# Modulation sums of a two-block network as rows in TensorE's 32-column tiles instead of folds on VectorE

## The chip, the core and the metric

One core of a Trainium2 chip runs the whole program in one launch. TensorE multiplies, VectorE and ScalarE work element by element (VectorE also sums and transposes blocks), GpSimd adds and issues DMAs, SyncE issues DMAs. The metric is the device time of one execution in microseconds (us); less is better.

## The reference, cut to what matters

A hybrid network over 256 tokens of 2048 features: a first block (stick-breaking attention and retention, modulated by a vector `c`), then two further layers and a last norm. The change concerns the first block's modulation and norm:

```python
mod = jax.nn.silu(c) @ w_ada[layer] + b_ada[layer]      # w_ada: 2048 x 6144
shift, scale, gate = jnp.split(mod, 3, axis=-1)
h = rms_norm(x, norm_gain[layer]) * (1.0 + scale[:, None, :]) + shift[:, None, :]
proj = h @ w_in[layer]
...
x = x + (gate[:, None, :] * y).astype(x.dtype)
```

All of it is float32.

## The kernel before

**Products.** Every matrix product is cut into chunks of 1024 columns of weights (for instance 4 x 256 columns of four groups of 128 input features). SyncE loads a chunk into one of seven places of `raw` (L453, waiting until the chunk seven before is used). ScalarE writes its high half `w_hi` (`split_hi`, L469; five places, so it waits for the chunk five before), VectorE the low half `w_lo` (`split_lo`, L478), and TensorE multiplies high by high and low, low by high (L544 to L546 where the result is by tokens, L552 and L554 where it is by features). A finished block of the sum `psG` is taken out by ScalarE (L512, L513, L515, L519) and VectorE (L1357, L1374, L1385). ScalarE and VectorE are three chunks ahead of TensorE (`AHEAD`).

**The order of the work** is written by hand: each engine walks through the same list of chunks ("units"), and at each position (`p` even: in front of or within a chunk; odd: behind it) a hook may add other instructions. In the first 72 units (`mem_hook_1`, `mem_tail_hook` and `early_hook`) ScalarE and VectorE run the hook of unit u behind the split of chunk u + 3, TensorE its own behind the products of chunk u. What a hook waits for holds up all that its engine has queued behind it.

- Units 0 to 31 (`G_MEM`): keys and values of the memory; in units 4 to 18 sixteen pieces of `w_ada` (the first quarter) are multiplied by silu(c) and added on VectorE into `quarter_sum[0]`; units 17 to 21 square x for norm 1 on ScalarE (`norm_square`), VectorE adds the squares (`squares_added`), TensorE sums them over partitions behind unit 25 (`sum_squares`).
- The second quarter is added by VectorE for eight pieces and by TensorE for the other eight (`row_sums`: four 32-column tiles, each multiplying a piece of 256 columns by a 32-wide weight, so 32 equal rows in each of four quarters of the partitions). `columns_of_rows` then turns the rows into columns by two products with every 32nd column of `ident`. ScalarE copies the rows between the two (L913).
- Units 32 to 71 (`EARLY`): the first parts of the first block's projections. VectorE adds sixteen halves of `w_ada` into `ada_sum` (L1404). Then come `G_SBQK` and, with the attention between them, `G_SBV`, `G_RTQK` and `G_RTV`; in them VectorE adds the 32 pieces of the gate, sixteen for each half of its columns, into `gate_sum`. `G_SBZ` follows with the retention.
- A sum over partitions of a finished `*_sum` is a **fold**: VectorE transposes in 32x32 blocks (L1463, L1477) and reduces by 32 (L1464, L1478) into `folded`, and TensorE multiplies by `fold_to` (`unfold`, L2147), which leaves a column in each quarter; VectorE adds the bias quarter by quarter (`modulation`, L1498, or `gate_columns`, L1577). Folds: quarter 0 in unit 19 (unfolded behind unit 24), the halves in unit 34 of `EARLY` (behind unit 35), gate 0 behind `G_SBQK`, gate 1 in `G_SBZ` at p = 10.

## Time and profile before

| | us |
|---|---|
| timed runs | 1719.99, 1724.51, 1725.9 (median 1724.51) |
| the profiled execution | 1721.63 |
| its span, first to last instruction | 1719.8 |
| TensorE busy in it | 1686.9 |
| VectorE, ScalarE busy | 1300.7, 902.5 |
| granted clock, mean | 0.996 |

A line of the profile names an engine (PE is TensorE, PEld its weight loads, DVE VectorE, ACT ScalarE, POOL GpSimd, SP SyncE), the line of the kernel, the operation, the tile written and the tiles read. A float32 product is recorded as two matmuls. Idle time stands in brackets with what ended it. Idle time of an engine that is not the bottleneck costs nothing, and TensorE is the bottleneck here.

### The profile page before, as it was taken

Reading aid. Unit: us, or ns where it says so; the run is one execution under the profiler, and the core shown is the slowest. Engines: PE = TensorE matmul, PEld = TensorE weight load, DVE = VectorE, ACT = ScalarE, POOL = GpSimd, SP = SyncE. Lnnn points to the kernel's source line nnn. Section 1 sums busy time; section 2 is a strip of 40 time slices with the busy share of each in tenths; the row PEclk is TensorE's granted clock in tenths of the full one; section 3 lists DMA queues with packets and bytes.
Section 4 is the critical chain, followed back from the end, with each engine's and each line's share of the span. In section 5 each row is a group of like instructions: output and inputs, shape, how many; then the busy total and the mean of one; then the engine's idle time right before and its main releaser. Section 6 shows DMA issues by size and latency. Waiting matters only on the chain.

```text
span 1719.8 us, 24010 instructions
## 1 busy us (share of the span) xinstructions
PE 1686.9 (98%) x9489; PEld 1445.8 (84%) x9489; DVE 1300.7 (76%) x1637; ACT 902.5 (52%) x1180; POOL 155.6 (9%) x166
## 2 busy tenths in 40 slices
PE   8999999999999999999999999999999999999997
PEld 6777878888888888888888888888888888888886
DVE  7878998898888766888677778966566666778754
ACT  6344453544566545665345666744445445566643
POOL 1221101001010210101010010001111000000001
PEclk9999999999999999999999999999999999999999
DMA  9989989776555567667686556666667565454563
GB/s 344 375 298 323 379 268 330 257 226 186 153 163 184 185 188 199 188 185 221 177 226 197 165 166 173 196 186 192 187 192 196 169 200 143 140 138 138 172 190 110
DMA packets 312190, 356.99 MB, mean 208 GB/s; under 512 B 11408, under 2 KB 285072, under 8 KB 312080
## 3 DMA queue, kind: packets, MB, share of 16 engines
q1 hardware_dynamic: 295952, 296.24, 56.9%
q0 software_dynamic: 16128, 59.22, 10.1%
q8 instruction: 76, 1.25, 0.3%
q14 instruction: 34, 0.28, 0.1%
HBM read 353.29 MB, written 2.13 MB: 207 GB/s over the span
## 4 chain that ended last, share of the span: by engine, by line
PE 78%; DVE 11%; ACT 5%; DMA 3%; issue 2%; POOL 0%; SPq 0%; DVEq 0%; ACTq 0%; POOLq 0%
PE psG L552 45%; PE psG L554 22%; DVE w_lo L478 4%; ACT w_hi L469 2%; DMA raw<-in_mem_w 2%; PE psG L544 2%; PE psG L546 2%; PE psG L545 2%; DMA raw<-in_w_in 1%; DVE ada_sum L1404 1%; DVE P L1357 1%; PE psH L2124 0%; DVE W L2027 0%; PE psG L548 0%; DMA P<-in_memT 0%
## 5 line engine op out<-in xcount | busy, mean ns | idle before, releaser
L478 DVE TENSOR_TENSOR w_lo<-raw,w_hi 128x1024 fp32r<-128x1024 f32 (+1 forms) x556 | 681.5, 1239 | 204.6 <-ACT w_hi L469 203.0
L552 PE MATMUL psG<-xA,w_hi 128*128 128x512 f32 x2592 | 827.7, 401 | 4.2 <-DVE P L1357 3.2
L469 ACT ACTIVATE w_hi<-raw 128x1024 fp32r<-128x1024 f32 (+1 forms) x556 | 565.4, 1041 | 220.0 <-PE psG L554 147.8
L554 PEld LDWEIGHTS psG<-xA,w_lo 128*128 128x128 f32 x2592 | 487.6, 188 | 115.0
L554 PE MATMUL psG<-xA,w_lo 128*128 128x256 f32 x2592 | 510.7, 278 | 0.0
L552 PEld LDWEIGHTS psG<-xA,w_hi 128*128 128x128 f32 x2592 | 397.4, 189 | 14.3 <-issue 9.2
L552 PE MATMUL psG<-yP,w_hi 128*128 128x512 f32 x960 | 302.0, 396 | 0.3 <-DVE yP L1701 0.3
L554 PEld LDWEIGHTS psG<-yP,w_lo 128*128 128x128 f32 x960 | 180.3, 188 | 42.6
L554 PE MATMUL psG<-yP,w_lo 128*128 128x256 f32 x960 | 188.6, 278 | 0.0
L519 ACT ACTIVATE P<-psG 128x512 f32<-128x512 f32 x101 | 59.9, 593 | 199.1 <-PE psG L554 199.1
L1357 DVE TENSOR_TENSOR P<-psG,P 128x512 f32<-128x512 f32 (+2 forms) x103 | 70.3, 683 | 105.9 <-ACT P L519 105.9
L552 PEld LDWEIGHTS psG<-yP,w_hi 128*128 128x128 f32 x960 | 146.2, 189 | 0.5 <-DVE yP L1701 0.5
L670 POOL TENSOR_TENSOR W<-W 128x512 f32<-128x512 f32 x11 | 19.1, 1734 | 571.8 <-ACT W L775 571.8
L1385 DVE TENSOR_TENSOR xT<-psG,xT 128x512 f32<-128x512 f32 x30 | 20.7, 691 | 41.6 <-PE psG L554 41.1
L544 PE MATMUL psG<-w_hi,xA 128*128 128x512 f32 x128 | 51.2, 400 | 0.0
L546 PE MATMUL psG<-w_hi,xA 128*128 128x512 f32 x128 | 49.9, 390 | 0.0
L545 PE MATMUL psG<-w_lo,xA 128*128 128x512 f32 x128 | 49.9, 390 | 0.0
L552 PE MATMUL psG<-xQ,w_hi 128*128 128x512 f32 x144 | 45.3, 396 | 0.1
L552 PE MATMUL psG<-xM,w_hi 128*128 128x512 f32 x128 | 41.6, 407 | 3.6 <-DVE w_lo L478 3.6
L805 ACT ACTIVATE xA<-xT,vec 128x256 fp32r<-128x256 f32 x32 | 14.4, 502 | 51.8 <-DVE xT L1388 27.2
L1404 DVE SCALAR_TENSOR_TENSOR gate_sum<-gate_ring,silc,gate_sum 128x1024 f32<-128x1024 f32 x30 | 38.3, 1277 | 0.0
L1404 DVE SCALAR_TENSOR_TENSOR ada_sum<-half_ring,silc,ada_sum 128x2048 f32<-128x2048 f32 x15 | 35.2, 2345 | 0.0
(371 smaller groups left out, 1783.6 us busy)
## 6 DMA issues: line engine op xcount, KB each, us to landing
raw<-in_w_in SPq DMA_DIRECT2D x360, 512.0 KB, 3.8
raw<-in_w_out SPq DMA_DIRECT2D x128, 512.0 KB, 3.5
raw<-in_mem_w SPq DMA_DIRECT2D x32, 512.0 KB, 11.3
quarter_ring<-in_w_ada POOLq DMA_DIRECT2D x32, 512.0 KB, 7.1
half_ring<-in_w_ada POOLq DMA_DIRECT2D x16, 1024.0 KB, 8.7
gate_ring<-in_w_ada POOLq DMA_DIRECT2D x32, 512.0 KB, 5.2
raw<-in_w_uq SPq DMA_DIRECT2D x24, 384.0 KB, 3.3
raw<-in_w_ukv SPq DMA_DIRECT2D x32, 128.0 KB, 2.4
```

The lines of the kernel that those rows point to most:

```text
L469: nc.scalar.activation(high(n), low(n, raw), ACT.Copy).then_inc(hi_ready, 1)
L478: nc.vector.tensor_tensor(low(n), low(n, raw), high(n), ALU.subtract).then_inc(lo_ready, 1)
L519: nc.scalar.activation(g.dst(b), product(g, b, 0), ACT.Copy).then_inc(copied, 1)
L544: nc.tensor.matmul(out, x_hi, hi[:, w], start=first, stop=False)
L545: nc.tensor.matmul(out, x_hi, lo[:, w], start=False, stop=False)
L546: last = nc.tensor.matmul(out, x_lo, hi[:, w], start=False, stop=end)
L552: nc.tensor.matmul(psG[:, bank + f, :], hi[:, w], x, start=first, stop=False)
L554: last = nc.tensor.matmul(psG[:, bank + f, S:2 * S], lo[:, w], x[:, 0:S], start=False, stop=end)
L670: pair(nc.gpsimd.tensor_tensor(a[:, 0:512], a[:, 0:512], a[:, 512:1024], ALU.add))
L1357: ins = v.tensor_tensor(out, product(g, b, 1), out, ALU.add)
L1385: ins = v.tensor_tensor(x, src, x, ALU.add)
L1404: v.scalar_tensor_tensor(out=out, in0=src, scalar=scale, in1=out, op0=ALU.mult, op1=ALU.add).then_inc(ada_used, 1)
```

## The change

All five sums over partitions take the way of the second quarter. TensorE multiplies the finished sum by 32 columns of ones in four tiles (`row_sums_of_added`; 256 columns a tile, 512 for the halves), ScalarE copies the rows (`rows_copied`), TensorE turns them into columns (`columns_of_rows`; two turns, four for the halves), VectorE adds the bias in one instruction. The folds, `folded`, the matrix `make_fold_to` and the semaphore `ada_folded` go. Places: quarter 0, rows behind unit 22, copy in ScalarE's unit 24, columns behind TensorE's unit 24; halves, rows behind unit 34 of `EARLY`, copy in ScalarE's unit 35, columns behind unit 35; gate 0, rows behind the first chunk of `G_SBV`, copy ahead of ScalarE's next split, columns behind the third chunk; gate 1, rows behind the eighth chunk of `G_SBZ`, columns behind the ninth. The squares of norm 1 move on ScalarE from units 17, 18, 20, 21 to 17, 19, 21, 23 and their sums on VectorE from 18, 20, 21 to 18, 20, 22. The counts of `rows_used` that GpSimd's loads wait for are one higher, for the same events.

```diff
         work1 = sb("work1", [NP, 2048], place=in_p(FIRST_WORK))
+        row_buf = {1: quarter_rows[:, :], 2: quarter_rows[:, :], 3: work1[:, 0:512], 4: work1[:, 0:256], 5: work1[:, 0:256]}
+        ROWS = {1: 1, 2: 2 + QUARTERS - ADDED, 3: 3 + QUARTERS - ADDED, 4: 4 + QUARTERS - ADDED, 5: 5 + QUARTERS - ADDED}
...
                 if i >= ADDED + 6:
-                    pool.wait_ge(q["rows_used"], i - ADDED - 5)
+                    pool.wait_ge(q["rows_used"], i - ADDED - 4)
...
                 if j < 3:
-                    pool.wait_ge(q["rows_used"], (4, 6, 8)[j])
+                    pool.wait_ge(q["rows_used"], (5, 7, 9)[j])
...
+            def rows_copied(n, bank):
+                act.wait_ge(q["rows_used"], ROWS[n])
+                to = row_buf[n]
+                f(to, psH[:, bank, 0:to.shape[1]], ACT.Copy).then_inc(q["root_or_rows"], 1)
...
                     mem_root()
-                if unit in (17, 18, 20, 21):
+                if unit == 24:
+                    rows_copied(1, BA)
+                if unit in (17, 19, 21, 23):
                     act.wait_ge(loaded["x"], 64)
-                    norm_square(1, (17, 18, 20, 21).index(unit), xT)
+                    norm_square(1, (17, 19, 21, 23).index(unit), xT)
...
                 if unit == 4:
-                    act.wait_ge(q["rows_used"], QUARTERS - ADDED + 1)
-                    f(quarter_rows[:, :], psH[:, BA, 0:D_MODEL // 8], ACT.Copy).then_inc(q["root_or_rows"], 1)
+                    rows_copied(2, BA)
+                if unit == EARLY_UNITS - 5:
+                    rows_copied(3, BA)
...
                     f(sb_a[:, 512:1024], tiles(n * 2 + SBK, 2), ACT.Square).then_inc(q["sb_sq"], 1)
+                if p == 2 and n == 0:
+                    rows_copied(4, BD)
...
             def rt_hook(n, p):
+                if p == 1 and n == 1:
+                    rows_copied(5, BC)
...
                 if j == 0:
-                    dve.wait_ge(q["rows_used"], QUARTERS - ADDED + 1)
+                    dve.wait_ge(q["rows_used"], ROWS[2])
...
                 if i == KT:
-                    dve.wait_ge(q["ada_folded"], 3)
+                    dve.wait_ge(q["rows_used"], ROWS[4])
...
-            def fold(src, parts):
-                turned_sum = work1[:, 0:1024 * parts]
-                link(v.transpose(turned_sum, src))
-                v.reduce_sum(folded[:, 0:32 * parts], turned_sum.rearrange("p (b j) -> p b j", j=32), AX).then_inc(q["ada_folded"], 1)
-            def make_fold_to():
-                dve.wait_ge(loaded["con"], 16)
-                for a in range(4):
-                    quarter = slice(32 * a, 32 * a + 32)
-                    v.tensor_copy(fold_to[quarter, :].rearrange("p (b j) -> p b j", j=32),
-                                  ident[quarter, quarter].unsqueeze(1).broadcast_to([32, 4, 32]))
-            def quarter_fold():
-                dve.wait_ge(ada_used, KT)
-                link(v.transpose(fold_work.rearrange("p c n -> p (c n)"), quarter_sum[0].rearrange("p c n -> p (c n)")))
-                v.reduce_sum(folded[:, 0:32], fold_work.rearrange("p c (b j) -> p (c b) j", j=32), AX).then_inc(q["ada_folded"], 1)
-            def unfolded(parts, width, quarter):
-                return psH[32 * quarter:32 * quarter + 32, BD, 0:width].rearrange("p (c t q) -> p c t q", c=parts, q=4)[:, :, :, quarter]
...
-                def cols(x):
-                    return x.rearrange("p (c t) -> p c t", c=2)[:, :, t0:t0 + tiles]
-                if n == 2:
-                    ins = v.tensor_tensor(mod[:, 0:32].rearrange("p (c t) -> p c t", c=2)[:, :, t0:t0 + tiles]
-                                          .rearrange("p c (j h) -> p c j h", h=2),
-                                          psH[:, BD, 0:8].rearrange("p (h c j) -> p c j h", h=2, c=2),
-                                          V("b_ada", 0, 32).rearrange("p (c t) -> p c t", c=2)[:, :, t0:t0 + tiles]
-                                          .rearrange("p c (j h) -> p c j h", h=2), ALU.add)
-                else:
-                    for a in range(4):
-                        quarter = slice(32 * a, 32 * a + 32)
-                        ins = v.tensor_tensor(cols(mod[quarter, 0:32]), unfolded(2, 8 * tiles, a), cols(V("b_ada", 0, 32)[quarter]), ALU.add)
+                def by_turn(x):
+                    return x.rearrange("p (c t) -> p c t", c=2)[:, :, t0:t0 + tiles].rearrange("p c (j h) -> p c j h", j=2)
+                ins = v.tensor_tensor(by_turn(mod[:, 0:32]), psH[:, BD, 0:2 * tiles].rearrange("p (h c j) -> p c j h", c=2, j=2),
+                                      by_turn(V("b_ada", 0, 32)), ALU.add)
...
                     quarter_add(i)
-                if u == 13:
-                    make_fold_to()
-                if u in (18, 20, 21):
-                    squares_added(1, (18, 20, 21).index(u))
-                if u == 19:
-                    quarter_fold()
+                if u in (18, 20, 22):
+                    squares_added(1, (18, 20, 22).index(u))
...
                     half_add(HALF_AT[u])
-                if u == EARLY_UNITS - 6:
-                    dve.wait_ge(ada_used, ADDED + HALVES)
-                    fold(ada_sum.rearrange("p c n -> p (c n)"), 2)
...
-            def gate_fold(half):
-                dve.wait_ge(ada_used, ADDED + HALVES + KT * (half + 1))
-                fold(gate_sum[:, :], 1)
...
                 c = 32 + 8 * half
-                for a in range(4):
-                    quarter = slice(32 * a, 32 * a + 32)
-                    v.tensor_tensor(mod[quarter, c:c + 8].unsqueeze(1), unfolded(1, 32, a), V("b_ada", c, 8)[quarter].unsqueeze(1), ALU.add)
+                v.tensor_tensor(mod[:, c:c + 8].rearrange("p (a h) -> p a h", h=2),
+                                psH[:, (BD, BC)[half], 0:8].rearrange("p (h a) -> p a h", h=2),
+                                V("b_ada", c, 8).rearrange("p (a h) -> p a h", h=2), ALU.add)
             run(G_SBQK, gate_hook(G_SBQK))
-            gate_fold(0)
...
                 if p == 8:
-                    if n == 0:
-                        dve.wait_ge(q["ada_folded"], 3)
...
-            run(G_SBV, both(sb_hook, gate_hook(G_SBV)))
-            run(G_RTQK, both(lambda b, p: sb_hook(1 + b, p), gate_hook(G_RTQK), first_gate_hook))
+            run(G_SBV, both(sb_hook, gate_hook(G_SBV), first_gate_hook))
+            run(G_RTQK, both(lambda b, p: sb_hook(1 + b, p), gate_hook(G_RTQK)))
...
                     v.tensor_tensor(turned[up], q_and_k[low, :, 2 * n:2 * n + 2, :], sin4[low], ALU.mult).then_inc(q["rt_s"], 1)
-                if p == 10 and n == 0:
-                    gate_fold(1)
...
-            def unfold(n, parts, name):
-                pe.wait_ge(q["ada_folded"], n)
-                mm(psH[:, BD, 0:32 * parts], fold_to[:, :], folded[:, 0:32 * parts], start=True, stop=True).then_inc(q[name], 1)
-            def row_sums(src, weights, first, end):
-                piece = src.rearrange("p c n -> p (c n)")
+            def flat(x):
+                return x.rearrange("p c n -> p (c n)")
+            def row_sums(piece, weights, first, end, bank=BA):
+                cols = piece.shape[1] // 4
                 for a in range(4):
-                    ins = mm(psH[32 * a:32 * a + 32, BA, 0:256], weights, piece[:, 256 * a:256 * a + 256], start=first, stop=end)
+                    ins = mm(psH[32 * a:32 * a + 32, bank, 0:cols], weights, piece[:, cols * a:cols * a + cols], start=first, stop=end)
                 ins.then_inc(q["rows_used"], 1)
+            def row_sums_of_added(piece, used, bank):
+                pe.wait_ge(ada_used, used)
+                row_sums(piece, ones[:, 0:32], True, True, bank)
...
                         pe.wait_ge(q["silc_step"], 2)
-                        row_sums(quarter_ring[i % 6], silc[:, i - KT:i - KT + 1].broadcast_to([NP, 32]), i == ADDED, False)
+                        row_sums(flat(quarter_ring[i % 6]), silc[:, i - KT:i - KT + 1].broadcast_to([NP, 32]), i == ADDED, False)
...
                     pe.wait_ge(ada_used, ADDED)
-                    row_sums(quarter_sum[1], ones[:, 0:32], False, True)
-            def columns_of_rows():
-                pe.wait_ge(q["root_or_rows"], 3)
-                for h in range(2):
-                    ins = mm(psH[:, BD, 4 * h:4 * h + 4], quarter_rows[:, h * NP:h * NP + NP], ident[:, 0:NP:32], start=h == 0, stop=h == 1)
-                ins.then_inc(q["ada_cols"], 1)
+                    row_sums(flat(quarter_sum[1]), ones[:, 0:32], False, True)
+            def columns_of_rows(n, bank, name):
+                pe.wait_ge(q["root_or_rows"], 2 + n)
+                rows = row_buf[n]
+                turns = rows.shape[1] // NP
+                for h in range(turns):
+                    ins = mm(psH[:, bank, 4 * h:4 * h + 4], rows[:, h * NP:h * NP + NP], ident[:, 0:NP:32], start=h == 0, stop=h == turns - 1)
+                ins.then_inc(q[name], 1)
...
                     ins.then_inc(q["root_or_rows"], 1)
+                if u == 22:
+                    row_sums_of_added(flat(quarter_sum[0]), KT, BA)
                 if u == 24:
-                    unfold(1, 1, "ada_cols")
+                    columns_of_rows(1, BD, "ada_cols")
...
                     if p % 2 and u == 4:
-                        columns_of_rows()
+                        columns_of_rows(2, BD, "ada_cols")
+                    if p % 2 and u == EARLY_UNITS - 6:
+                        row_sums_of_added(flat(ada_sum), ADDED + HALVES, BA)
                     if p % 2 and u == EARLY_UNITS - 5:
-                        unfold(2, 2, "ada_cols")
+                        columns_of_rows(3, BD, "ada_cols")
...
             def sb_hook(n, p):
-                if p == 5 and n == 1:
-                    unfold(3, 1, "gate_cols")
+                if p == 5 and n == 0:
+                    columns_of_rows(4, BD, "gate_cols")
+                if p == 1 and n == 0:
+                    row_sums_of_added(gate_sum[:, :], ADDED + HALVES + KT, BD)
...
             def rt_hook(n, p):
+                if p == 15 and n == 0:
+                    row_sums_of_added(gate_sum[:, :], ADDED + HALVES + GATES, BC)
                 if p == 1 and n == 1:
-                    pe.wait_ge(q["rt_ln"], 1)
-                    unfold(4, 1, "gate_cols")
+                    columns_of_rows(5, BC, "gate_cols")
```

## Rows read from the trace of the kernel before

**Rows 1.** The page, section 1: busy time, share of the span, instructions
```profile
PE 1686.9 (98%) x9489; PEld 1445.8 (84%) x9489; DVE 1300.7 (76%) x1637; ACT 902.5 (52%) x1180; POOL 155.6 (9%) x166
```

**Rows 2.** Waits of TensorE, 0 to 520 us: waiting, released by: total, times, longest
```profile
PE psG L552 <- DVE w_lo L478: 3.6, 2, 1.9
PE psG L552 <- DVE P L1357: 3.2, 2, 2.5
PE psH L2147 <- DVE folded L1464: 2.3, 1, 2.3
```

**Rows 3.** Stretches: length, busy of PE, PEld, DVE, ACT, POOL, clock, DMA, GB/s
```profile
80.00:100.00 20.00, 15.72 (x72) 12.81 (x71) 15.57 (x18) 10.94 (x14) 2.31 (x4) 0.91 0.86 283
...
220.00:240.00 20.00, 17.71 (x79) 14.40 (x78) 19.16 (x28) 8.62 (x14) 1.61 (x3) 1.00 0.77 252
```

**Rows 4.** Timeline of ScalarE: start, duration, what, [idle before, releaser]
```profile
83.76 1.06 ACT L775 ACTIVATE W<-xT 128x1024 f32<-128x1024 f32 x1 [2.87 <-DVE W L1436]
...
88.64 1.06 ACT L775 ACTIVATE W<-xT 128x1024 f32<-128x1024 f32 x1 [2.87 <-DVE W L1436]
89.60 1.99 ACT L469 ACTIVATE w_hi<-raw 128x1024 fp32r<-128x1024 f32 x2
...
92.64 2.94 ACT L469 ACTIVATE w_hi<-raw 128x1024 fp32r<-128x1024 f32 x3
```

**Rows 5.** Timeline of VectorE, the sum of squares in unit 20
```profile
82.06 0.68 DVE L1432 TENSOR_TENSOR W<-W 128x512 f32<-128x512 f32 x1
```

**Rows 6.** Timeline of TensorE, 82 to 97 us
```profile
82.29 0.47 PE L544 MATMUL psG<-w_hi,xM 128*128 128x512 f32 x1 [0.68 <-DVE w_lo L478]
...
87.17 0.70 PE L552 MATMUL psG<-xM,w_hi 128*128 128x512 f32 x2 [1.89 <-DVE w_lo L478]
...
92.05 0.70 PE L552 MATMUL psG<-xM,w_hi 128*128 128x512 f32 x2 [1.71 <-DVE w_lo L478]
...
94.85 1.05 PE L552 MATMUL psG<-xM,w_hi 128*128 128x512 f32 x2
...
96.13 0.96 PE L2130 MATMUL psH<-W,con 128*128 128x256 f32 x2
```

**Rows 7.** DMA issues of 67 to 69.5 us (us to landing), and SyncE's timeline there
```profile
raw<-in_mem_w SPq DMA_DIRECT2D x1, 512.0 KB, 17.3
...
67.78 0.37 SPq L453 DMA_DIRECT2D raw<-in_mem_w  x1
```

**Rows 8.** Timeline of TensorE and ScalarE, rows and columns of the second quarter
```profile
109.89 1.07 PE L2153 MATMUL psH<-quarter_ring,silc 128*32 128x256 f32 x16
...
110.89 0.73 PE L552 MATMUL psG<-xM,w_hi 128*128 128x512 f32 x2
...
132.05 0.37 ACT L913 ACTIVATE quarter_rows<-psH 128x256 f32<-128x256 f32 x1
...
134.54 0.50 PE L2171 MATMUL psH<-con,quarter_rows 128*128 128x4 f32 x4
134.91 0.70 PE L552 MATMUL psG<-xA,w_hi 128*128 128x512 f32 x2
```

**Rows 9.** Timeline of VectorE and TensorE around the fold of the halves
```profile
220.25 2.35 DVE L1404 SCALAR_TENSOR_TENSOR ada_sum<-half_ring,silc,ada_sum 128x2048 f32<-128x2048 f32 x1
...
225.99 2.29 DVE L1464 TENSOR_REDUCE folded<-work 128x64 f32<-128x2048 f32 x1
...
228.33 0.43 PE L2147 MATMUL psH<-folded,fold_to 128*128 128x64 f32 x2 [2.29 <-DVE folded L1464]
228.57 0.48 PE L544 MATMUL psG<-w_hi,xA 128*128 128x512 f32 x1
```

**Rows 10.** Timeline of TensorE: a 512-column f32 pair, and the last gate's columns
```profile
311.40 1.02 PE L2224 MATMUL psH<-W,con 128*128 128x512 f32 x2
...
449.67 0.30 PE L2147 MATMUL psH<-folded,fold_to 128*128 128x32 f32 x2
449.81 0.70 PE L552 MATMUL psG<-xA,w_hi 128*128 128x512 f32 x2
```

More of the change, by code:

```diff
@@ L191, in build @@
         fold_to = sb("fold_to", [NP, NP])
-        folded = sb("folded", [NP, 64])
         def in_p(tile):
@@ L252, in build @@
             "rt_t0 rt_s rt_qk rt_D rt_z rt_at rt_o rt_os rt_vc rt_sq rt_var rt_ln rt_rs rt_y "
-            "f1_yz f1_y f1_hi f1_lo dt_step ada_folded rows_used root_or_rows mem_k "
+            "f1_yz f1_y f1_hi f1_lo dt_step rows_used root_or_rows mem_k "
             "cv_acc cv_tap cv_a cv_e cv_l cv_b cv_s cv_done xt xd_done "
```

## The prediction

> **What bounds the kernel now.** I read the page first: of a span of 1719.8 us TensorE is busy 1686.9 [rows 1], so nothing is worth more than what TensorE stands idle or spends on small products. Then the waits of TensorE in the first 520 us, where the change lies [rows 2]: 3.6 us behind low halves of weights (L478), 3.2 us behind block sums (L1357), 2.3 us behind `folded` (L1464). The change touches the 2.3 us and, through the squares of norm 1, the 3.6. By stretches [rows 3] the granted clock is 0.91 from 80 to 100 us, around the pair of 1.9 and 1.7 us, and 1.00 around the 2.3 us: behind the pair TensorE ran for a while at 1.2 GHz instead of 2.4, seen as pairs of 512-column products of 1.05 us instead of 0.70 and less [rows 6]. Last I read ScalarE, VectorE and TensorE side by side from 79 to 98 us [rows 4 to 6].
>
> **Stage one, units 18 to 25 (79 to 98 us).** ScalarE now squares group 2 of norm 1 in unit 20, but only once VectorE has added group 1 in the same unit: it idles 2.87 us and starts at 83.76; the same again one unit on, at 88.64 [rows 4]. So the high half of chunk 25 starts at 89.60 and TensorE waits 1.89 us ahead of chunk 24 and 1.71 us ahead of chunk 25, which starts at 92.05 [rows 4, 6].
> The change puts the squares into units 17, 19, 21, 23 and VectorE's sums into 18, 20, 22, and takes the fold (transposition and reduction) out of unit 19. I ran the new order by hand. Chunk 25 was asked for at 67.78 and took 17.3 us: there at 85.1; chunk 24 is there earlier [rows 7]. ScalarE: square 2 waits for VectorE's sum of unit 20, which begins at 82.06 in any case behind low 23 [rows 5], and starts at 83.76 as before; then high 25 at 85.1 (before 89.60). VectorE: low 25 from 86.15 to 87.3, quarter addition 16 (under 0.7), then the sum of group 2. From its first addition to ScalarE's square is 1.70 (82.06 to 83.76). ScalarE has high 26 done at 87.3, waits, squares group 3 at 89.65, takes the two halves of the token block (L512, L513), and starts high 27 at 91.75. Before, from the square at 88.64 over two splits and the block to high 27 at 92.64 are 4.00 [rows 4]; the two splits fall away (1.9), leaving 2.1.
> TensorE: chunk 23 at 82.29 as before, 2.8 us long like every chunk (12 products of 0.23 us or four steps of 0.70), chunk 24 right behind it at 85.12 instead of 87.17 [rows 6], done at 87.95. Here stands the new wait. `columns_of_rows(1)` sits behind chunk 24 (unit 24) and needs ScalarE's copy `rows_copied(1)`, which ScalarE issues in its own unit 24, behind high 27. The old `unfold` in that place waited for a fold of unit 19, long done. High 27 takes 0.95 to the next start, the copy 0.37 [rows 8]: it is there at 93.1. TensorE stands from 87.95 to 93.1, 5.1 us in one piece where it stood 1.89 + 1.71; queued behind it are all products from chunk 25 on. The columns take 0.37 and the load of their weights about 0.2, so chunk 25 starts at 93.65: **+1.6 us** against 92.05. The clock fell once before; I expect it to fall once again at the same price, so 0. The quarter's row sums behind chunk 22 hide in the wait of 0.68 that ends at 82.29 [rows 6]. TensorE needs the sum of squares only behind chunk 25, and group 3 is done at 90.7.
> From there to 222 us TensorE waits only for what its own earlier blocks released, so the +1.6 passes through. The stall of 2.5 us behind a block sum [rows 2] stays: rows and columns of the second quarter are as they were.
>
> **Prices of the new pieces.** Two row sums of 256 columns start at 109.89 and the next product at 110.89 [rows 8]: 1.00 for 16 passes of 256 columns, where a single pair of 512 takes 1.02 [rows 10], so the four tiles were at work at once. A lone one lies between 0.5 and 1.0; I take 0.6. Columns of two turns start at 134.54, the next product at 134.91 [rows 8]: 0.37. The old `unfold` costs 0.14 (449.67 to 449.81) and with 64 columns 0.24 (228.33 to 228.57) [rows 9, 10]. Row sums of 512 columns do not occur before. A pair of 512-column f32 products is 1.02 [rows 10]; four in column tiles at once are that, 1.07 with their entry. Bounds: 0.6 (as narrow ones) and 4.1 (four one behind another). I take 1.07, as the narrow ones ran at once. Columns of four turns: 0.74, bounds 0.5 and 1.0.
> On mode switches the Trainium skill speaks against the change: its page "TensorEngine Tiling (Array Packing)", section "Tiling Modes", says that changing the tiling mode drains TensorE. The rows leave no room for a large drain, since 1.00 holds two calls and the way in and out [rows 8]; by a drain that weighed on every lone call, each would be nearer 1.0 and the sum 1.2 us larger.
>
> **Halves (units 34 to 36, 220 to 229 us).** Before: last addition of the halves at 220.25, then a low half, the transposition, and the reduction of 2.29 us from 225.99, all on VectorE; TensorE waits 2.29 us and starts chunk 68 at 228.57, where it could have started it at 225.88: 2.69 lost [rows 9]. After: row sums behind chunk 66, at 223.2 + 1.6 = 224.8. They find the addition done (220.25 + 2.35 = 222.6, and 224.2 if VectorE is shifted by the whole 1.6). 1.07 for them, the copy hides beside chunk 67, 0.74 for the columns: 1.81. Net **-0.9** (bounds -1.6 and +2.4). Late next is nothing: the low half of chunk 71 is needed three chunks on.
>
> **Gates.** The two folds were on VectorE beside a busy TensorE, and [rows 2] has no wait for them, so their going gives nothing. TensorE gets 0.6 + 0.37 for 0.14, twice: **+1.7** (bounds +1.4 and +2.5). The first gate's copy now stands on ScalarE ahead of the split of the fourth chunk on and of the root of the scores; both waited for TensorE's chunk behind it anyway. Cover lost there would cost up to a chunk's 2.7 us. One modulation addition in place of four is hidden on VectorE.
> Here too a rule of the skill speaks against the change: "VectorE: DVE Perf Modes", section "Rules for kernel authors", calls VectorE's own transpose the fastest for 32x32 blocks. The rows agree for the gates, where the fold costs TensorE 0.14 and the rows 0.97; keeping those two folds would make the sum 1.7 smaller.
>
> **Sum.** +1.6 - 0.9 + 1.7 = +2.4 us. The profiled execution took 1721.63 (span 1719.8): 1724.0. The timed runs are 1719.99, 1724.51 and 1725.9; the mean of all four is 1723.0, the profiled one 1.4 under it, the median 1.5 over it. I put the sum on the mean: **1725.4 us**, no change that can be measured (0.3%, 5.2 us, is about the least that can).
>
> **Rivals.**
> The copy is in time. If ScalarE reaches its unit 24 without waiting for the sum of group 2, high 27 starts at about 87.8, the copy ends at 89.2 and chunk 25 starts near 89.7, 2.35 us earlier than before, and the clock does not fall. That fall cost about 1.7, an estimate: chunk 25 took 4.1 us (92.05 to 96.13, [rows 6]) instead of 2.8, and I add 0.4 for the sum of squares behind it, which began at that clock. Sum -2.35 - 1.7 - 0.9 + 1.7 = -3.3: 1719.7, and 1718.0 if the second fall of the clock, behind the 2.5 us stall, goes too. For it: the waits of 2.87 us in [rows 4] are what the new spacing loosens. Against it: VectorE's sum still lies behind low 25, which the landing at 85.1 puts at 87.3.
> The clock (slower). One stall of 5.1 us leaves TensorE at 1.2 GHz for longer than two short ones. Each further stretch like the one before costs 1.7; two more give 2.4 + 3.4 = +5.8: 1728.8. It decides where the stall is over 3 us and products stay at 1.05 beyond 99 us. For it: 0.91 behind the pair of stalls [rows 3]. Against it: 1.00 around a stall of 2.29 us.
> The stage is neutral. Chunk 24's gain and the wait behind it cancel, chunk 25 starts at 92: +0.8, 1723.8.
>
> **Chances.** Forecast 0.43 (own range 1722 to 1729), copy in time 0.27, clock 0.20, neutral 0.10. More than 0.3% faster needs the first rival and the second fall gone, or a low run: 0.15. More than 0.3% slower: nearly all of the clock rival and a little of the forecast, 0.19. Within: 0.66. The range reaches to the ends of both rivals, 1718 to 1730.
>
> **What would show it.** The first columns of rows near 93 us, behind a wait of TensorE of some 5 us for ScalarE's copy (right) or of under 1.5 us (copy in time). Products at 1.05 us beyond 99 us (clock). No wait at 225.9, but 1.8 us of rows and columns there; 0.8 us more at either gate. Wrong if the tiles are not at work at once (over 3 us near 224), or if TensorE waits at the gates.

## The result, and the profile after

The changed kernel takes 1725.97 us (median of 20 runs, 1723.8 to 1727.71), the kernel before beside it 1723.3 us (20 runs, 1719.74 to 1727.84): a ratio of 1.0014, with a 95% interval of 1.0008 to 1.0021. That is 2.7 us slower by the medians and within the 0.3% that the prediction calls no change. The profiled executions stand to each other alike: a span of 1722.6 us against 1719.8.

The page of the changed kernel, section 1, and the three longest of its waits of TensorE from 0 to 520 us (waiting instruction, released by: total us, times, longest):

```profile
span 1722.6 us, 24076 instructions
PE 1692.4 (98%) x9533; PEld 1448.9 (84%) x9533; DVE 1286.9 (75%) x1613; ACT 904.3 (52%) x1184; POOL 155.5 (9%) x166
```

```profile
PE psH L2142 <- ACT quarter_rows L886: 4.0, 1, 4.0
PE psG L545 <- DVE w_lo L479: 3.6, 5, 1.3
PE psG L553 <- DVE P L1371: 3.2, 2, 2.5
```

VectorE lost 13.8 us of work [rows 1], and nobody gains by it; TensorE has 5.5 us more. Of the waits in [rows 2], the 3.6 us behind low halves in the by-feature chunks (now L553) are gone, and so are the 2.3 us behind `folded`. In their place stands one new wait of 4.0 us: the first `columns_of_rows`, for ScalarE's copy. (The 3.6 us in the second line are waits of the by-token chunks, L545, that come and go between traces of all kernels.)

The stage from 80 to 100 us on TensorE (start, duration, what, idle before and its releaser), with the stretches (length, busy of PE, PEld, DVE, ACT, POOL, clock, DMA share, GB/s) under it:

```profile
81.61 0.64 PE L2117 MATMUL psH<-quarter_sum,con 128*32 128x256 f32 x8
82.18 0.50 PE L545 MATMUL psG<-w_hi,xM 128*128 128x512 f32 x1
...
85.04 0.61 PE L553 MATMUL psG<-xM,w_hi 128*128 128x512 f32 x2
...
92.00 1.01 PE L2142 MATMUL psH<-con,quarter_rows 128*128 128x4 f32 x4 [4.03 <-ACT quarter_rows L886]
92.88 1.20 PE L553 MATMUL psG<-xM,w_hi 128*128 128x512 f32 x2
...
95.58 1.05 PE L553 MATMUL psG<-xM,w_hi 128*128 128x512 f32 x2
...
97.83 0.59 PE L2096 MATMUL psH<-W,con 128*128 128x256 f32 x2
```

```profile
90.00:95.00 5.00, 3.00 (x10) 2.71 (x11) 4.05 (x4) 3.84 (x6) 1.29 (x2) 0.56 0.83 292
95.00:100.00 5.00, 5.00 (x22) 4.32 (x22) 3.80 (x4) 0.00 (x0) 1.60 (x3) 0.76 0.60 193
```

Chunk 24 starts at 85.04 right behind chunk 23, without the wait of 1.89 us of [rows 6]. Then TensorE stands 4.03 us in one piece, and runs on at 1.2 GHz: pairs of 1.05 us and a granted clock of 0.56 and 0.76. Chunk 25 takes 4.95 us (92.88 to 97.83), where in [rows 6] it took 4.08. ScalarE's timeline shows why the copy comes so late:

```profile
82.17 1.06 ACT L776 ACTIVATE W<-xT 128x1024 f32<-128x1024 f32 x1
83.92 1.06 ACT L470 ACTIVATE w_hi<-raw 128x1024 fp32r<-128x1024 f32 x1 [0.69 <-DMA raw<-in_mem_w]
85.79 1.06 ACT L470 ACTIVATE w_hi<-raw 128x1024 fp32r<-128x1024 f32 x1 [0.80 <-DMA raw<-in_mem_w]
88.52 1.06 ACT L776 ACTIVATE W<-xT 128x1024 f32<-128x1024 f32 x1 [1.67 <-DVE W L1450]
89.48 0.67 ACT L513 ACTIVATE memkv<-psG,col 128x512 f32<-128x512 f32 x1
...
90.62 1.05 ACT L470 ACTIVATE w_hi<-raw 128x1024 fp32r<-128x1024 f32 x1
91.57 0.38 ACT L886 ACTIVATE quarter_rows<-psH 128x256 f32<-128x256 f32 x1
```

The DMA of chunk 25's weights, asked for at 68.08, with its us to landing:

```profile
raw<-in_mem_w SPq DMA_DIRECT2D x1, 512.0 KB, 15.8
```

ScalarE's high half of chunk 23, some chunks earlier:

```profile
78.24 1.06 ACT L470 ACTIVATE w_hi<-raw 128x1024 fp32r<-128x1024 f32 x1 [2.07 <-DMA raw<-in_mem_w]
```

The row sums end at 82.25. The copy of 0.38 us stands behind two high halves that wait for DMAs, a square that waits for VectorE, a block and one more high half.

The halves and the gates, TensorE again, answer to [rows 9] and the last two of [rows 10]:

```profile
224.59 1.06 PE L2117 MATMUL psH<-ada_sum,con 128*32 128x512 f32 x8
225.59 0.50 PE L545 MATMUL psG<-w_hi,xA 128*128 128x512 f32 x1
...
228.45 0.95 PE L2142 MATMUL psH<-con,work 128*128 128x4 f32 x8
229.25 0.49 PE L545 MATMUL psG<-w_hi,xA 128*128 128x512 f32 x1
...
309.74 0.39 PE L547 MATMUL psG<-w_hi,xA 128*128 128x512 f32 x1
310.06 0.64 PE L2117 MATMUL psH<-gate_sum,con 128*32 128x256 f32 x8
310.63 0.50 PE L545 MATMUL psG<-w_hi,xA 128*128 128x512 f32 x1
310.97 0.39 PE L546 MATMUL psG<-w_lo,xA 128*128 128x512 f32 x1
...
452.09 0.50 PE L2142 MATMUL psH<-con,work 128*128 128x4 f32 x4
452.45 0.70 PE L553 MATMUL psG<-xA,w_hi 128*128 128x512 f32 x2
```

From start to next start, a row sum of 256 columns costs 0.57 us, one of 512 columns 1.00, columns of two turns 0.36, of four turns 0.80. These are not yet their whole price, since the products beside them start later too. In a steady run such products start 0.23 us apart. The row sum starts 0.32 us behind the product ahead of it (309.74 to 310.06), and the product behind it takes 0.34 to the next start (310.63 to 310.97): 0.2 more, so 0.77 and 1.20 in full. Columns have only the later start behind them: 0.45 and 0.9 in full, and the old `unfold` in the same way 0.22. The wait of 2.29 us for the fold is gone.

### The profile page after: what moved, and what is told of

It is laid out like the page before. It is cut to its first block, busy times and chain, and to the rows that moved or that the text cites. A ratio compares the mean times of both kernels' runs of the same rounds, so it can differ in the third digit from the quotient of the medians.

```text
span 1722.6 us, 24076 instructions
## 1 busy us (share of the span) xinstructions
PE 1692.4 (98%) x9533; PEld 1448.9 (84%) x9533; DVE 1286.9 (75%) x1613; ACT 904.3 (52%) x1184; POOL 155.5 (9%) x166
## 4 chain that ended last, share of the span: by engine, by line
PE 80%; DVE 10%; ACT 5%; issue 2%; DMA 2%; POOL 0%; SPq 0%; DVEq 0%; ACTq 0%; POOLq 0%
PE psG L553 45%; PE psG L555 22%; DVE w_lo L479 4%; ACT w_hi L470 2%; PE psG L545 2%; PE psG L547 2%; PE psG L546 2%; DMA raw<-in_mem_w 2%; DVE P L1371 1%; PE psH L2090 0%; DVE W L1993 0%; PE psG L549 0%; DVE P L1379 0%; PE psH L2348 0%; PE psH L2117 0%
## 5 line engine op out<-in xcount | busy, mean ns | idle before, releaser
L553 PE MATMUL psG<-xA,w_hi 128*128 128x512 f32 x2592 | 827.8, 401 | 4.2 <-DVE P L1371 3.2
L553 PEld LDWEIGHTS psG<-xA,w_hi 128*128 128x128 f32 x2592 | 397.3, 189 | 14.8 <-issue 9.6
L553 PE MATMUL psG<-yP,w_hi 128*128 128x512 f32 x960 | 302.0, 396 | 0.3 <-DVE yP L1667 0.3
L553 PEld LDWEIGHTS psG<-yP,w_hi 128*128 128x128 f32 x960 | 146.2, 189 | 0.5 <-DVE yP L1667 0.5
L545 PE MATMUL psG<-w_hi,xA 128*128 128x512 f32 x128 | 51.6, 403 | 0.0
L553 PE MATMUL psG<-xQ,w_hi 128*128 128x512 f32 x144 | 45.3, 396 | 0.0
L553 PE MATMUL psG<-xM,w_hi 128*128 128x512 f32 x128 | 42.2, 413 | 0.0
```

The lines of the kernel that those rows point to most:

```text
L545: nc.tensor.matmul(out, x_hi, hi[:, w], start=first, stop=False)
L553: nc.tensor.matmul(psG[:, bank + f, :], hi[:, w], x, start=first, stop=False)
```

## The experiments

Eleven runs, ten kernels. To compare traces I use four marks on TensorE: the first product of chunk 24 (from there on, differences in how fast the execution started drop out), of unit 32, of `G_SBQK`, and of the layer behind the first block (its input is `yP`). Behind the last mark all traces take the same time, 1195.3 to 1195.6 us. The lengths of the stretches between the marks, the time lost at 1.2 GHz (length of a 5 us stretch times what the granted clock lacks of 1, summed from 85 to 100 and from 140 to 155 us), and the ratios:

| kernel | chunk 24 to unit 32 | unit 32 to `G_SBQK` | `G_SBQK` to `yP` | lost near 93, near 148 | median us | ratio to before (95%) |
|---|---|---|---|---|---|---|
| before | 30.49 | 121.92 | 284.89 | 1.7, 1.7 | 1723.3 | 1 |
| changed | 33.96 | 121.28 | 286.82 | 3.4, 1.75 | 1725.97 | 1.0014 (1.0008 to 1.0021) |
| columns late | 27.26 | 120.03 | 286.81 | 0, 0 | 1717.5 | 0.9965 (0.9952 to 0.9978) |
| old spacing | 33.67 | 121.28 | 286.83 | 3.4, 1.7 | 1726.51 | 1.0011 (1.0003 to 1.002) |
| spacing alone | 26.97 | 122.39 | 284.87 | 0, 1.75 | 1719.67 | 0.9976 (0.9966 to 0.9986) |
| wait filled | 31.48 | 121.34 | 286.83 | 0, 1.7 | 1723.94 | 1.0 (0.999 to 1.0009) |
| halves alone | 28.92 | 121.41 | 284.98 | 1.7, 1.7 | 1721.11 | 0.9984 (0.9975 to 0.9993) |
| halves alone, again | 28.91 | 121.0 | 284.98 | 0, 0 | 1721.53 | 0.9989 (0.998 to 0.9998) |
| spacing and halves | 27.04 | 123.3 | 284.98 | 0, 1.7 | 1718.78 | 0.9964 (0.9951 to 0.9978) |
| gates alone | 28.9 | 123.54 | 286.75 | 0, 1.7 | 1725.53 | 1.0008 (1.0 to 1.0017) |
| late, old spacing | 29.35 | 119.79 | 286.82 | 0, 0 | 1722.79 | 0.999 (0.9982 to 0.9999) |
| copy early | 27.26 | 121.28 | 286.82 | 0, 1.7 | 1719.59 | 0.9971 (0.9961 to 0.9982) |
| best mix | 27.19 | 119.74 | 284.96 | 0, 0 | 1716.88 | 0.9958 (0.9945 to 0.997) |

The kernel before ran beside each group: 1723.64 us beside the first group (columns late, old spacing, spacing alone, wait filled), 1724.84 beside the second (halves alone, spacing and halves, gates alone, late with old spacing), 1724.08 beside the third (halves again, copy early, best mix); the ratios are the ones to compare across groups.

One column needs care: time lost at 1.2 GHz is not always time lost by the kernel. In the first trace of the halves alone the clock fell behind the first wait of 1.88 us (chunk 24, pairs of 1.05 us), and the slower chunk ate most of the wait ahead of chunk 25; its first stretch, 28.92 us, equals that of the two other traces with the old stage, in which the clock did not fall (28.91, 28.9). In the trace of before it fell behind the second wait, and the stretch is 30.49.

My theory from the two traces: the stage below 100 us has gained its 3.6 us by the new spacing and gives them back, with more in clock, at the wait for the copy; the gates cost, the halves gain a little.

**Columns late.** The first columns behind unit 26 instead of 24, nothing else.

```diff
-                if u == 24:
-                    columns_of_rows(1, BD, "ada_cols")
                 if u == 25:
                     sum_squares(1)
+                if u == 26:
+                    columns_of_rows(1, BD, "ada_cols")
```

> The changed kernel with one edit: the first columns of rows stand behind TensorE's unit 26 instead of 24, so that ScalarE's copy (ready at 92.0 us) is no longer waited for. Theory (the wait for ScalarE's copy in unit 24 and the slower clock behind it make stage one dearer by about 7 us than it need be): no wait of 4 us at 92; chunk 25 starts near 88.0 instead of 92.9 and chunk 26 near 92.8 instead of 99.8; clock 1.00 from 80 to 100 us; 5 to 7 us less than the changed kernel, so 1719 to 1721, faster than before by 2 to 4 us. Rival (the stage is neutral, the change costs only by its additional work on TensorE): 1725 to 1727, the time of the changed kernel.

8.5 us less than the changed kernel by the medians, and faster than before. TensorE and ScalarE in it:

```profile
85.36 0.70 PE L553 MATMUL psG<-xM,w_hi 128*128 128x512 f32 x2
...
91.01 0.59 PE L2096 MATMUL psH<-W,con 128*128 128x256 f32 x2
...
95.95 0.51 PE L2142 MATMUL psH<-con,quarter_rows 128*128 128x4 f32 x4
```

```profile
80.02 1.06 ACT L470 ACTIVATE w_hi<-raw 128x1024 fp32r<-128x1024 f32 x1 [1.89 <-DMA raw<-in_mem_w]
...
92.55 0.39 ACT L886 ACTIVATE quarter_rows<-psH 128x256 f32<-128x256 f32 x1
```

The copy comes even later than in the changed kernel (91.57), yet TensorE has passed chunk 25 by then and asks for the rows only at 95.95. Chunks 24 and 25 take 5.65 us together, there is no wait in the stage and the clock stays up. The stretch to unit 32 is 6.7 us shorter than in the changed kernel: 4.03 for the wait, 2.1 for chunk 25 at full clock (2.8 instead of 4.95), 0.5 for the columns (0.36 instead of 0.88 at 1.2 GHz). Another 1.25 us is the second stretch, in which the clock did not fall in this trace.

**Old spacing.** The changed kernel with the squares back where they were, in units 17, 18, 20, 21 (sums in 18, 20, 21).

```diff
-                if unit in (17, 19, 21, 23):
+                if unit in (17, 18, 20, 21):
...
-                if u in (18, 20, 22):
-                    squares_added(1, (18, 20, 22).index(u))
+                if u in (18, 20, 21):
+                    squares_added(1, (18, 20, 21).index(u))
```

> The changed kernel with the squares of norm 1 put back to units 17, 18, 20, 21 (and their sums to 18, 20, 21). Theory (the copy is late because it stands in ScalarE's unit 24 behind the split of chunk 27, whichever units the squares have): by the spacings of the trace the copy is done at 92.3 in either order; chunk 25 starts at 92.7 to 93.2; 1725.5 to 1726.5, no difference from the changed kernel. Rival (the square in unit 23 makes the copy late): the copy is there by 91 and the time is 1.5 to 3 us under the changed kernel, 1723 to 1724.5.

```profile
87.61 0.70 PE L553 MATMUL psG<-xM,w_hi 128*128 128x512 f32 x2 [1.88 <-DVE w_lo L479]
...
94.45 1.02 PE L2142 MATMUL psH<-con,quarter_rows 128*128 128x4 f32 x4 [3.81 <-ACT quarter_rows L886]
```

The wait ahead of chunk 24 is back, and the wait for the copy stands behind it all the same. By time it equals the changed kernel: with the columns behind unit 24 the spacing is worth nothing that the times show (in this one trace the columns come at 94.45 instead of 92.00, 0.5 us of it because chunk 23 had already begun later). My theory was wrong on the copy: it had it done at 92.3 in either order, and with the old spacing it is done at 94.40.

**Late, old spacing.** Both edits at once.

> The changed kernel with the first columns behind unit 26 and the squares back in units 17, 18, 20, 21. Theory (with the copy out of the way the spacing decides: both short stalls of the kernel before come back): waits of 1.5 to 2 us ahead of chunks 24 and 25, the clock falls once near 93 us, 4 to 6 us more than with the columns late and the new spacing: 1722 to 1724. Rival (the new spacing gives nothing by itself): 1717 to 1718.

The edits are the two diffs above. 0.999 against the 0.9965 of the late columns: once the copy no longer stands in the way, the spacing is worth some 4 us (1.7 ahead of chunk 24 and 2.1 in the stretch behind it by the traces). The two waits are those of [rows 6]:

```profile
87.18 0.70 PE L553 MATMUL psG<-xM,w_hi 128*128 128x512 f32 x2 [1.73 <-DVE w_lo L479]
...
92.06 0.70 PE L553 MATMUL psG<-xM,w_hi 128*128 128x512 f32 x2 [1.86 <-DVE w_lo L479]
```

**Spacing alone.** The kernel before with the new spacing, all sums still folds.

```diff
-                if unit in (17, 18, 20, 21):
+                if unit in (17, 19, 21, 23):
...
-                if u in (18, 20, 21):
-                    squares_added(1, (18, 20, 21).index(u))
+                if u in (18, 20, 22):
+                    squares_added(1, (18, 20, 22).index(u))
```

> The kernel before with only the squares two units apart; folds and unfold stay. Theory (the spacing takes away both stalls of TensorE, and nothing takes their place where no copy is waited for): chunk 24 starts near 85.1, chunk 25 near 88.1 instead of 92.05, the clock stays at 1.00 to 100 us, 5 to 6 us less than before: 1717 to 1719. Rival (the stalls come from the arrival of the weights, and the spacing is neutral): 1722 to 1724.

0.9976: 4 us faster, where I had expected 5 to 6. This is what the spacing gives in the kernel before, where `unfold` behind unit 24 finds its fold long done:

```profile
86.37 0.62 PE L552 MATMUL psG<-xM,w_hi 128*128 128x512 f32 x2
...
89.16 0.30 PE L2147 MATMUL psH<-folded,fold_to 128*128 128x32 f32 x2
```

```profile
85.00:90.00 5.00, 5.00 (x29) 4.31 (x28) 3.97 (x5) 2.96 (x3) 0.72 (x1) 1.00 1.09 347
90.00:95.00 5.00, 5.00 (x29) 4.39 (x28) 4.01 (x6) 4.44 (x6) 0.72 (x1) 1.00 0.94 322
```

No wait in either stretch, clock 1.00. So the changed kernel holds one good edit, and it spends its gain elsewhere.

**Wait filled.** The changed kernel with sixteen products of the zero matrix ahead of the first columns, in the 4 us in which TensorE stands. It tells the price of the idle time from the price of the clock.

```diff
                 if u == 24:
+                    for _ in range(16):
+                        mm(psH[:, BD, 0:NP], fold_to[:, :], fold_to[:, :], start=True, stop=True)
                     columns_of_rows(1, BD, "ada_cols")
```

> The changed kernel with 16 products of zeros by zeros (128 x 128 by 128 columns, as in its warm-up) on TensorE between chunk 24 and the first columns: they fill the 4.0 us in which TensorE waits for the copy and add nothing to the result. Theory (of the 7 us the wait is some 4 and the slower clock behind it some 2.5): the copy is there at the same 92, but the products of chunk 25 take 0.63 instead of 1.05 a pair, chunk 26 starts at 97.2 to 97.8 instead of 99.8, 2 to 3 us less than the changed kernel: 1723 to 1724. Rival (the clock costs nothing here, or falls anyway): 1726, the time of the changed kernel.

```profile
87.87 3.73 PE L2162 MATMUL psH<-fold_to 128*128 128x128 f32 x32
92.05 0.61 PE L2142 MATMUL psH<-con,quarter_rows 128*128 128x4 f32 x4 [0.45 <-ACT quarter_rows L886]
...
95.41 0.59 PE L2096 MATMUL psH<-W,con 128*128 128x256 f32 x2
```

The copy comes at the same moment (columns at 92.05 instead of 92.00), so nothing of the wait is saved, but the clock stays at 2.4 GHz and the norm's sum starts at 95.41 instead of 97.83. 2.5 us less in the stretch, 2.0 by the medians: that much of the changed kernel's time is clock, in an edit that only adds work.

**Copy early.** The changed kernel with `rows_copied(1)` in ScalarE's unit 22, the columns left behind TensorE's unit 24.

```diff
-                if unit == 24:
+                if unit == 22:
                     rows_copied(1, BA)
```

> The changed kernel with ScalarE's copy of the first rows moved ahead by two of its units (22 instead of 24), the columns still behind chunk 24. Theory (the 4.0 us wait is the copy's place in ScalarE's order, behind weights that come by DMA): the rows are there at 82.2 us and the copy ends before 88 us, TensorE doesn't wait at the columns, chunk 25 begins some 4 us sooner, the clock doesn't fall at 80 to 100 us, and the time is that of the late columns, 1717.5 us, or with one clock stretch left 1719, ratio 0.9965 to 0.9975. Rival A (the wait has only moved: ScalarE now stands at the rows, the squares and weight copies behind it come late, and TensorE waits for them for 1 to 2 us): 1721 to 1723 us. Rival B (what the late columns gained was the mode switch at chunk 24 and not the wait): 1725.5 us, ratio 1.0013.

```profile
87.59 0.70 PE L553 MATMUL psG<-xM,w_hi 128*128 128x512 f32 x2 [0.20 <-DVE w_lo L479]
...
90.45 0.50 PE L2142 MATMUL psH<-con,quarter_rows 128*128 128x4 f32 x4
90.81 0.70 PE L553 MATMUL psG<-xM,w_hi 128*128 128x512 f32 x2
...
93.68 0.59 PE L2096 MATMUL psH<-W,con 128*128 128x256 f32 x2
```

```profile
87.99 0.36 ACT L886 ACTIVATE quarter_rows<-psH 128x256 f32<-128x256 f32 x1
```

The copy is done 2.1 us before TensorE asks, the wait is gone with the columns in their old place, and what TensorE pays is 0.36 us. From chunk 24 to unit 32 it takes 27.26 us, to the hundredth what the late columns take, and 0.9971 by time. Two different ways round the same wait give the same stretch, so neither the products nor the change of tiling behind unit 24 was what cost; it was ScalarE's order. (This trace lost 3.4 us at 1.2 GHz near its start, from 5 to 20 us, behind a first wait of 3.07 us; no other trace did so there, and no step of the reasoning rests on that stretch.)

**Halves alone.** The kernel before with the halves as rows: row sums behind unit 34 of `EARLY`, copy in ScalarE's unit 35, columns behind unit 35.

```diff
-                if u == EARLY_UNITS - 6:
-                    dve.wait_ge(ada_used, ADDED + HALVES)
-                    fold(ada_sum.rearrange("p c n -> p (c n)"), 2)
...
+                    if p % 2 and u == EARLY_UNITS - 6:
+                        pe.wait_ge(ada_used, ADDED + HALVES)
+                        halves = ada_sum.rearrange("p c n -> p (c n)")
+                        for a in range(4):
+                            ins = mm(psH[32 * a:32 * a + 32, BA, 0:512], ones[:, 0:32], halves[:, 512 * a:512 * a + 512], start=True, stop=True)
...
                     if p % 2 and u == EARLY_UNITS - 5:
-                        unfold(2, 2, "ada_cols")
+                        columns_of_rows(work1[:, 0:512], 4)
```

> The kernel before with only the halves as rows and columns on TensorE (quarter 0 and both gates stay folds on VectorE, squares as before). Theory (TensorE lost 2.69 us at the fold and now spends 1.09 on rows and 0.80 on columns, as in the changed kernel): the first product of the later part (239.58 before) comes 0.8 us earlier, 1722.5 to 1723.3, not to be told from before by its time alone. Rival (VectorE, freed of 4.6 us, gives more): 2 us or more earlier there, 1721.5 or less.

> The kernel before with the halves alone as rows, as once already (there 1721.11 us, ratio 0.9984, 0.9975 to 0.9993). It is repeated for the size: the traces of the first time show 0.5 us less between the first xA product and the first of G_SBQK, the times 2.7 us. If the edit is worth what the stretches show, the ratio is 0.9993 to 0.9997 (0.5 to 0.9 us); if it is worth what the times showed, 0.9984 again.

0.9984 and 0.9989, some 2 to 3 us, where I had 0.9. The edit can't be what shortens the first stretch, which ends before it (28.92 and 28.91, as with the gates alone). In the second stretch this one and the changed kernel give 121.4 and 121.3, the three kernels that keep the fold give 121.92, 122.39 and 123.54, with waits for the fold of 2.29, 1.76 and 2.92 us: a gain of 0.6 to 2.2 by the trace that it is compared with. The repeat shows 121.0, but in it the clock did not fall near 148 us, and TensorE waited for the last addition of the halves:

```profile
222.07 1.07 PE L2211 MATMUL psH<-ada_sum,con 128*32 128x512 f32 x8 [0.70 <-DVE ada_sum L1407]
```

So the sign is settled, and about 1 us of gain is seen. Where the rest of the times' 2 to 3 us comes from stays open: by its time the first run is where the rival had put it (VectorE's freed time gives more, 1721.5 us or less), and the traces neither show that nor exclude it. The interval of the second time (0.998 to 0.9998, 0.3 to 3.4 us) holds both.

**Spacing and halves.** The kernel before with the new spacing and the halves as rows.

> The kernel before with the squares two units apart and the halves as rows; quarter 0 and the gates stay folds. Theory (the parts add up: spacing -4, halves -0.3 to -0.8, gates and the quarter's copy left out): 1718 to 1719.5, and the time up to the later part (235.7 with the spacing alone) shorter by 0.3 to 0.8; if the clock does not fall near 145 us either, 1.3 less. Rival (the columns-late kernel at 1717.5 owes its time to the rows of the gates, which free VectorE): this one is slower than it by 2 us.

1718.78 us, 0.9 under the spacing alone (2 us by the ratios), which the intervals don't tell apart. Its trace has a wait of 1.48 us of its own at 132.7 us, behind weights that landed late, and its second stretch (123.3) says nothing on the halves.

**Gates alone.** The kernel before with both gates as rows.

```diff
-            gate_fold(0)
...
-                if p == 10 and n == 0:
-                    gate_fold(1)
...
-                if p == 5 and n == 1:
-                    unfold(3, 1, "gate_cols")
+                if p == 5 and n == 0:
+                    gate_cols(4, BD)
+                if p == 1 and n == 0:
+                    gate_rows(ADDED + HALVES + KT, BD)
...
+                if p == 15 and n == 0:
+                    gate_rows(ADDED + HALVES + GATES, BC)
                 if p == 1 and n == 1:
-                    pe.wait_ge(q["rt_ln"], 1)
-                    unfold(4, 1, "gate_cols")
+                    gate_cols(5, BC)
```

> The kernel before with only the two gates as rows and columns. Theory (each gate gives TensorE 0.66 to 0.77 of rows and 0.36 to 0.47 of columns for the 0.14 of the old product, and the freed VectorE gives nothing back): the last products of the first block come 1.7 to 2.0 us later (524.5 before), 1725 to 1725.6. Rival (VectorE freed of 4.9 us pays it back): 1722 to 1723.5.

1.0008 by time. The third stretch is 286.75 us instead of 284.89. Over all thirteen traces this stretch knows two lengths: 284.87 to 284.98 in the six kernels and repeats that keep the gates' folds, 286.75 to 286.83 in the seven that don't. The gates cost 1.9 us, and no wait is among it: twice 0.57 + 0.36 less twice 0.14 makes 1.6 from start to next start, and with the later starts of the products beside them twice 0.77 + 0.45 less twice 0.22 makes 2.0.

**Best mix.** The kernel before with the spacing, quarter 0 as rows with its columns behind unit 26, and the halves as rows; the gates stay folds. Against the changed kernel:

```diff
-                if u == 24:
-                    columns_of_rows(1, BD, "ada_cols")
+                if u == 26:
+                    columns_of_rows(quarter_rows[:, :], 3)
...
-                if p == 5 and n == 0:
-                    columns_of_rows(4, BD, "gate_cols")
-                if p == 1 and n == 0:
-                    row_sums_of_added(gate_sum[:, :], ADDED + HALVES + KT, BD)
+                if p == 5 and n == 1:
+                    unfold(1, 1, "gate_cols")
```

> The kernel before with three edits: the norm's squares two units apart, quarter 0 as rows with its columns behind chunk 26, and the halves as rows; the gates stay folds on VectorE. It is the changed kernel with late columns, less the gates' part. Theory (the gates' rows cost 1.9 us between the first product of G_SBQK and the first yP product, and this comes back in full at the end): 284.9 us between these two marks instead of 286.8, and a time 1.9 us under that of the late columns' 1717.5, 1715.6 us, ratio to the kernel before 0.9952 (0.994 to 0.9965). Rival A (the stretch is shorter but another wait takes the time back): 1717.5 us, ratio 0.9965. Rival B (the fold of the gates has its own wait again and the clock falls in one stretch more): 1719 us.

1716.88 us, 0.9958 (0.9945 to 0.997): faster than both kernels, by 7.2 and by some 9 us. The gates' stretch is 284.96, as the theory has it; against the late columns the ratio is 0.0007 lower (1.2 us), in the span 2.3 us. The theory had 1.9 (1715.6 us), and the intervals of the two kernels overlap, so the gain over the late columns is shown by the stretch and not by the times. Its stage has no wait:

```profile
85.24 0.62 PE L552 MATMUL psG<-xM,w_hi 128*128 128x512 f32 x2
...
90.82 0.60 PE L2132 MATMUL psH<-W,con 128*128 128x256 f32 x2
...
95.76 0.51 PE L2174 MATMUL psH<-con,quarter_rows 128*128 128x4 f32 x4
```

## Why the prediction was right

It foresaw +2.4 us on a mean of 1723.0 and gave 1725.4; measured are 1725.97 and +2.7. The direction, the place of each cost and the signs were right. In stage one the number came out by luck: the copy came 1.15 us sooner than foretold, the clock cost 1.7 us that were put at nothing, and the two errors cancelled.

- **Chunk 24's start** was put at 85.12 and is 85.04. The two old waits, 3.6 us, are gone, as the spacing alone confirms.
- **The wait for `rows_copied(1)`** is there, in one piece, at the place foretold. Its end was put at 93.1 and is 91.95, its length at 5.1 and is 4.03. The step that missed is the landing of chunk 25's weights, "there at 85.1" by the 17.3 us of the trace before. Here they took 15.8 us and were there at 83.9; the high half began at 83.92, VectorE's low half at 85.02 instead of 86.15, and the rest of the chain ran as foretold, 1.1 us sooner. "Square 2 starts at 83.76 as before" missed too: it started at 82.17, since chunk 23 also landed sooner (high half at 78.24, in the trace before at 79.83), and VectorE's sum began at 80.47 instead of 82.06 [rows 5]. The fold that left unit 19 is not the reason: before, the fold and the high half of chunk 23 ended at the same moment (80.89). The trace of the columns late, with the same order on ScalarE and VectorE, has chunk 23's high half at 80.02, the square at 83.95 and the copy's end at 92.94, next to the foretold 93.1. A landing read from one trace is good to some 1.5 us here.
- **The clock** "falls once again at the same price, so 0" was wrong. The stretch lost 3.4 us instead of 1.7; chunk 25 took 4.95 us instead of 4.08 and the columns 0.88 instead of 0.36. That is half of the rival that I gave 0.20: one further loss of 1.7 us, not two. "Wait filled" shows its price, 2.0 to 2.5 us with the columns.
- **Together** chunk 25 starts 0.83 us later than before (foretold 1.6), and the norm's sum behind it 1.70 later (97.83 against 96.13); at unit 32 it is 1.34. Right in size, by a sooner copy and a longer slow stretch. It is also measured against one trace of before, whose stretch from chunk 24 is 30.49; against the 28.9 of the three other traces with the old stage it would be about 2.9.
- **The row sums of quarter 0 behind chunk 22** were called hidden, and they are: chunk 23 starts at 82.18 instead of 82.29.
- **Prices.** Row sum 0.6, measured 0.57; 512-wide 1.07, measured 1.00; two turns 0.37, measured 0.36; four turns 0.74, measured 0.80. The four tiles do run at once. The 1.02 of a pair of 512 columns [rows 10] was its duration and not its price: two such pairs start 0.86 apart (310.54 to 311.40). What these prices left out are the later starts of the products beside them: in full 0.77 for a lone row sum and 1.20 for two in a row (109.57 to 111.46, less 0.69 for the products' own steps). The Trainium skill's page "TensorEngine Tiling (Array Packing)", section "Tiling Modes", says that TensorE is drained at a change of mode. The trace agrees that something is paid for each call: the way in and out is 2 x 0.77 - 1.20 = 0.34 us, part of which (up to 0.1) also stands behind columns, which change no mode. Start to next start alone shows 0.14 of it.
- **Halves** -0.9, measured -0.64 in the second stretch of the two traces. The 1.81 of rows and columns is 1.80 from start to next start and 2.1 in full; the fold's 2.69 is 2.8 with the later start behind its product. That leaves -0.7. In other traces the fold's wait varies between 1.76 and 2.92.
- **Gates** +1.7, measured +1.93, and no cover was lost: the first gate's copy (310.77) ran beside TensorE. That the fold was the cheaper way here is what this stretch and the best mix show. The Trainium skill's "VectorE: DVE Perf Modes", section "Rules for kernel authors", calls VectorE's own transposition the fastest for such blocks. That is not what decided: no run here has the transposition by another way, and the whole fold of quarter 0 before took VectorE 1.24 + 1.22 us (78.40, 79.67), longer than rows, copy and columns together (0.57 + 0.38 + 0.36). It costs less because it runs beside TensorE, which pays only the product behind it.
- **The sum by the marks**: from the start of chunk 23 to the first product on `yP` are 444.92 us (82.18 to 527.10) against 442.18 (82.29 to 524.47), +2.74, where the steps foretold +2.4. With stretches that differ by 1.6 us between traces of the same stage, an agreement this close is partly chance.

What the experiments add: the chief rival, that the copy is in time, was a matter of one line. With the copy two units up, or the columns two units down, the change makes the kernel 0.3% faster, near the 1719.7 that this rival was given.

## What to carry to other kernels

Where work moves from one engine to a chain over two, the small step between (here a copy of 0.38 us) takes its place in an order written for other things; look at what stands ahead of it there, DMAs and other engines' results included, and either move it up or ask for its result later. Test the parts of a change apart: here one part gained 4 us, one cost 1.9, and one misplaced hook hid both. And a fold on an engine that has time cost TensorE here only the small product behind it, although its own instructions were the longer way, so moving it to the engine that bounds the kernel must pay for itself in waits removed: it did for the halves, not for the gates. For each small call count the later starts of its neighbours too: here they were 0.2 us beside each row sum.

## What the runs showed of the hardware

- What is lost at 1.2 GHz came in portions: about 1.7 us, or 3.4 behind the two waits of 4 us (3.81 and 4.03). Outside these stretches it came once near the start (3.4) and once near 40 us (1.7, in "wait filled"). With the old stage, waits of 1.7 to 1.9 us ahead of chunks 24 and 25, it fell behind the second in the trace of before, behind the first in that of the halves alone, and not at all in those of the repeat, of the gates alone and of the late columns with old spacing. Between 141 and 151 us all thirteen traces have a wait of 2.50 to 2.53 us, and the clock fell behind it in nine and not in four. The repeat and its first run are the same kernel:

```profile
90.00:95.00 5.00, 3.29 (x21) 2.87 (x20) 3.65 (x4) 5.00 (x7) 0.72 (x1) 1.00 0.44 152
```

  This row of the repeat holds the second wait, of 1.71 us, at a clock of 1.00. One trace thus doesn't tell whether a wait of that size costs clock as well; the waits of 4 us did so in both traces that had one.
- Products of a matrix of zeros kept the clock up over the wait (1.00 from 80 to 100 us in the trace with the wait filled), and the kernel was 2 us faster for them.
- Going into the four 32-column tiles and out again costs 0.34 us at most for a single call, by the difference above; 0.2 of it shows only in the starts of the products beside the call.
